# The opening of a two-block transformer kernel: conditioning weights loaded at once and made the stationary operand, normalized tiles scaled by two engines, their transposes placed between the groups of the first projection

## What is computed

```
mod_x = silu(c)     @ w_ada[l] + b_ada[l]      # 1024 -> 6 * 1024, for the tokens
mod_c = silu(c_ctx) @ w_ada[l] + b_ada[l]      # the same for the context
sh1, sc1, g1, sh2, sc2, g2 = split(mod, 6)
h_x = layer_norm(x)   * (1 + sc1) + sh1
h_c = layer_norm(ctx) * (1 + csc1) + csh1
p_x = h_x @ w_in                               # 1024 -> 544 + 1280 + 3 * 1024 columns
p_c = h_c @ w_in
```

## Time and profile before

| | us |
|---|---|
| median of 3 runs | 3383.12 |
| lowest and highest | 3379.35, 3383.62 |
| the profiled execution, its device time | 3381.08 |
| its span in the profile | 3379.0 |
| PE busy (x15388 matmuls) | 3080.0 (91%) |
| DVE busy | 2036.5 (60%) |
| ACT, POOL busy | 1028.9, 1001.6 (30% each) |

### The profile page before, as it was taken

One profiled execution on the slowest core, in us unless ns is written; L12 is line 12 of the kernel. 1 busy time (PEld: TensorE's weight loads), 2 busy tenths in 40 slices (PEclk: granted clock), 3 DMA queues, 4 the chain that ended last, 5 costly groups with the idle time before them and its releaser, 6 DMA issues.

```text
span 3379.0 us, 38543 instructions
## 1 busy us (share of the span) xinstructions
PE 3080.0 (91%) x15388; PEld 2491.5 (74%) x15388; DVE 2036.5 (60%) x3032; ACT 1028.9 (30%) x1799; POOL 1001.6 (30%) x754
## 2 busy tenths in 40 slices
PE   6998889999999999989899998899998887989798
PEld 3985767888488888869576676588878866787576
DVE  4576775555665555482677554666665856667354
ACT  3125773000231112131367200322222135421352
POOL 1003776552210000010078675200001135531262
PEclk9999999999999999989899999899998988999799
DMA  6411003433322121123101466132212310122100
GB/s 206 154 57 29 10 29 94 111 107 111 112 75 75 50 75 52 73 64 137 28 1 38 127 178 209 50 117 100 100 50 94 110 50 1 39 76 101 50 1 25
DMA packets 206353, 267.76 MB, mean 79 GB/s; under 512 B 29296, under 2 KB 133696, under 8 KB 205536
## 3 DMA queue, kind: packets, MB, share of 16 engines
q1 hardware_dynamic: 204096, 265.30, 24.4%
q10 hardware_dynamic: 2080, 0.01, 0.0%
HBM read 254.65 MB, written 10.52 MB: 78 GB/s over the span
## 4 chain that ended last, share of the span: by engine, by line
PE 38%; DVE 6%; ACT 2%; issue 2%; POOL 2%; DMA 1%; SPq 0%; DVEq 0%; POOLq 0%
PE ps L373 14%; PE ps L2010 5%; PE ps L2020 4%; PE ps L2500 2%; PE ps L1329 2%; PE ps L1792 1%; PE ps L1312 1%; PE ps L2830 1%; PE ps L1282 1%; PE ps L1094 1%; PE ps L2775 1%; DVE U L2945 1%; PE ps L3184 1%; DVE U L1439 0%; PE ps L3136 0%
## 5 line engine op out<-in xcount | busy, mean ns | idle before, releaser
L752 POOL TENSOR_TENSOR ht_lo<-HT,ht_hi 128x1024 fp32r<-128x1024 f32 x28 | 67.6, 2415 | 1075.0 <-DVE X L710 629.5
L2010 PE MATMUL ps<-ht_hi,w_hi 128*128 128x512 f32 (+1 forms) x832 | 286.9, 345 | 18.5 <-POOL ht_lo L752 9.8
L2010 PE MATMUL ps<-ht_lo,w_hi 128*128 128x512 f32 (+1 forms) x832 | 285.8, 343 | 0.0
L2010 PE MATMUL ps<-ht_hi,w_lo 128*128 128x512 f32 (+1 forms) x832 | 285.6, 343 | 0.0
L2020 PE MATMUL ps<-w_hi,a_hi 128*128 128x512 f32 x640 | 251.0, 392 | 4.3 <-DVE a_lo L2135 4.3
L2020 PE MATMUL ps<-w_lo,a_hi 128*128 128x512 f32 x640 | 249.9, 390 | 0.0
L2020 PE MATMUL ps<-w_hi,a_lo 128*128 128x512 f32 x640 | 249.7, 390 | 0.0
L373 PE MATMUL ps<-w_lo,ht_hi 128*128 128x320 f32 (+2 forms) x800 | 245.8, 307 | 0.0
L1496 POOL TENSOR_TENSOR p_lo<-ring,p_hi 128x512 fp32r<-128x512 f32 x156 | 199.9, 1292 | 102.7 <-DVE p_hi L1451 78.1
L595 DVE SCALAR_TENSOR_TENSOR U<-U,stat 128x512 f32<-128x512 f32 x224 | 218.8, 977 | 12.1 <-DMA U<-w_ada_dram 2.4
L373 PE MATMUL ps<-gate_ht_hi,gate_w_hi 128*128 128x512 f32 (+1 forms) x576 | 213.7, 371 | 12.1 <-POOL w_lo L1678 6.4
(11 more groups left out here) (427 smaller groups left out, 8232.9 us busy)
## 6 DMA issues: line engine op xcount, KB each, us to landing
ring<-w_dram SPq DMA_DIRECT2D x30, 2048.0 KB, 7.9
U<-w_ada_dram SPq DMA_DIRECT2D x80, 512.0 KB, 3.6
ring<-w_in_dram SPq DMA_DIRECT2D x48, 512.0 KB, 6.5
ring<-w_in_dram SPq DMA_DIRECT2D x8, 1280.0 KB, 6.0
ring<-a_w_in_dram SPq DMA_DIRECT2D x8, 1280.0 KB, 6.7
ring<-w_ada_dram SPq DMA_DIRECT2D x4, 2048.0 KB, 10.6
hi_scratch<-ht_hi SPq DMA_DIRECT2D x2, 3072.0 KB, 10.0
gate_ht_hi<-hi_scratch SPq DMA_DIRECT2D x8, 768.0 KB, 4.6
```

The source lines that it names most:

```text
L752: pool.tensor_tensor(HT_LO[:, :, tokens], HT[:, :, tokens], HT_HI[:, :, tokens].bitcast(F32), ALU.subtract).then_inc(ht_ready.sem, 1)
L2010: last = pe.matmul(ps[:, g % 4, 0:c1 - c0], lhsT, rhs, start=(k + j == 0), stop=(k == KD - 1 and j == 2))
```

## The change

`w_ada[0]`'s four blocks go to four places in `U` (`ADA_W`) and are asked for at the start, ahead of `w_in`; `ctx` is asked for between the second and the third. The weights become the stationary operand: for each of 16 blocks of 128 output columns, eight matmuls with the two columns of `sil` as the moving operand (new line 514), whose sums stand as columns in PSUM at once. The copies and the 16 small transposes go. The biases are added first (`ada_biases`). Tiles 0 and 1 are transposed between the blocks, tiles 2 to 5 ahead of groups 0 to 3 of A0. ACT scales the first four of a tile's eight feature pieces and DVE the other four (`place_half`, new line 818), interleaved with the splitting of A0's and A1's weights. `XNS` moves, so that the projection's output doesn't overwrite it. In `gemm` the units of `Macs` shift by one slot for the projection: unit u has its `pieces` behind the split of slot u+1 and its `pe` after group 0 of slot u+2, and what is left over stands behind the projection. Line numbers after line 217 differ by 2 to 32.

```diff
-        def gemm(G, mms, evac, depth, ..., pieced=None):
+        def gemm(G, mms, evac, depth, ..., pieced=None, beside=None):
-                                if macs and g == (2 if G == 3 else 1):
-                                    macs.pe(pe, i * 2 + s - 1)
+                                if macs and g == (2 if pieced else 1):
+                                    macs.pe(pe, i * 2 + s - (1 if pieced else 2))
...
+                                if beside:
+                                    beside(eng, i * 2 + s, 0)
                                 eng.wait_ge(ring_full[s].sem, i * (16 * parts) + ring_full[s].n + 16 * parts)
                                 for q in range(pieces):
+                                    if beside and q:
+                                        beside(eng, i * 2 + s, q)
...
                                 if macs and name[s] == "vector":
-                                    macs.take(eng, i * 2 + s - 1)
-                                    macs.pieces(eng, i * 2 + s, 0, 4)
+                                    macs.take(eng, i * 2 + s - 2)
+                                    macs.pieces(eng, i * 2 + s - 1, 0, 4)
...
-        MODROW = U[0:2, 6 * D:8 * D]
+        ADA_W = [view(at, KD, 512) for at in (8448, 12544, 4096, 0)]
...
+                    for c in range(4):
+                        if c == 2:
+                            sp.dma_start(X[:, XT:NT, :], A["ctx"]...).then_inc(ctx_loaded.sem, 16)
+                        sp.dma_start(ADA_W[c], rows(A["w_ada"][0])[:, :, c * 512:(c + 1) * 512]).then_inc(ada_loaded[c].sem, 16)
                     first_loads(sp, lambda s: None)
-                    sp.dma_start(X[:, XT:NT, :], A["ctx"]...).then_inc(ctx_loaded.sem, 16)
...
+        def ada_first(p):
+                    pe.wait_ge(sil_ready.sem, 1)
+                    for c in range(4):
+                        if c >= 2:
+                            turn_tile(pe, p, c - 2, XNS[:, c - 2, :], 2 * (c % 2))
+                        pe.wait_ge(ada_loaded[c].sem, 16)
+                        for j in range(4 * c, 4 * c + 4):
+                            for k in range(KD):
+                                last = pe.matmul(ps[:, 5, 2 * j:2 * j + 2], ADA_W[c][:, k, j % 4 * P:(j % 4 + 1) * P],
+                                                 sil[:, k, :], start=(k == 0), stop=(k == KD - 1))
+                    last.then_inc(mod_turned.sem, 1)
...
-        XNS = view(0, NT, D)
+        XNS = view(27984, NT, D)
...
-                        place_tile(act, p, 0, 0, t, 2 * (t % 2))
+                        place_tile(act, p, 0, 0, t, 2 * (t % 2), HALF)
+                        act.wait_ge(half_placed.sem, t + 1)
                         round_tile(act, p, t)
...
+        def place_half(dve, p, t):
+            dve.wait_ge(mod_ready.sem, 1)
+            dve.wait_ge(turn_done.sem, p.turned + t + 1)
+            for k in range(HALF, KD):
+                last = dve.tensor_scalar(HT[:, k, tokens], ps[:, 2 * (t % 2) + k // 4, k % 4 * P:(k % 4 + 1) * P],
+                                         modc[:, 0, KD + k, who:who + 1], modc[:, 0, k, who:who + 1], ALU.mult, ALU.add)
+            last.then_inc(half_placed.sem, 1)
...
             if macs:
+                macs.pe(nc.tensor, 2)
+                macs.take(nc.vector, 2)
+                macs.pieces(nc.vector, 3, 0, 4)
                 macs.pe(nc.tensor, 3)
                 macs.take(nc.vector, 3)
                 macs.all_taken(nc.tensor)
...
             def ready(pe, g):
+                if l == 0 and g + 2 < NT:
+                    pe.wait_ge(half_placed.sem, g + 1)
+                    turn_tile(pe, now, g + 2, XNS[:, g + 2, :], 2 * (g % 2))
                 pe.wait_ge(ht_ready.sem, now.ht + g + 1)
```

More of the change, by code:

```diff
@@ L217, in build @@
         bias_loaded = signal("bias_loaded")
+        ada_loaded = [signal(f"ada_loaded{c}") for c in range(4)]
+        half_placed = signal("half_placed")
         sil_ready = signal("sil_ready")
@@ L316, in first_loads, with gemm @@
                         d.then_inc(ring_full[s].sem, 16)
-        def gemm(G, mms, evac, depth, split=None, join=True, ready=None, loads=None, macs=None, behind=None, between=None, pieced=None):
+        def gemm(G, mms, evac, depth, split=None, join=True, ready=None, loads=None, macs=None, behind=None, between=None, pieced=None, beside=None):
             n, parts, issue = streams[at_stream[0]]
@@ L726, in place_tile @@
             act.wait_ge(turn_done.sem, p.turned + t + 1)
-            for k in range(KD):
+            for k in range(n):
                 last = act.activation(HT[:, k, tokens], ps[:, bank + k // 4, k % 4 * P:(k % 4 + 1) * P], ACT.Identity,
@@ L804, in first_ht, with half_beside, piece, project @@
             return p
+        def place_half(dve, p, t):
+            who = 0 if t < XT else 1
+            tokens = slice(t * P, (t + 1) * P)
+            dve.wait_ge(mod_ready.sem, 1)
[4 more added lines that the diff above has]
+            last.then_inc(half_placed.sem, 1)
+        def half_beside(p):
+            before = {0: (0,), 1: (1,), 3: (2,)}
+            def piece(dve, u, q):
+                if u == 0:
+                    for t in before.get(q, ()):
+                        place_half(dve, p, t)
+                if u == 1 and q == 0:
+                    for t in range(3, NT):
+                        place_half(dve, p, t)
+            return piece
         HT_HI = rounded_view("ht_hi", "U", at_ot, KD, T)
         PROJECT_W = [rounded_view(f"project_w_hi{s}", "U", at_xn + D + s * KD * 320, KD * 320) for s in range(SLOTS)]
-        def project(nt, width, col, dst, join=True, ready=None, macs=None):
+        def project(nt, width, col, dst, join=True, ready=None, macs=None, beside=None):
             def mms(s, g, d):
```

36 lines of the change are left out of this document (10 added, 26 removed).

## The result

| | median us (range) | ratio to before, 95% interval |
|---|---|---|
| before | 3381.23 (3373.94 to 3383.62) | |
| changed kernel | 3402.55 (3399.78 to 3405.98) | 1.0066 [1.005, 1.0082] |
| forecast | 3411, range 3380 to 3418 | |

The change makes the kernel slower by 21 us. The profiled executions say the same: 3400.7 us of span against 3379.0, +21.7. The forecast's sum was +28.8.

The account below looks back on a forecast made before the run. The prediction took the opening as one chain: conditioning product, scales, six tiles, projections. 24.3 - 6.9 + 11.4 = +28.8 on 3381.1 gave 3409.9; going halfway to a median 2.0 higher, it said 3411 us, range 3380 to 3418.

Parts of the forecast that it names:

- The conditioning product and the clock: Opening: product with stationary weights takes 54.5 us at 1.2 GHz, so the scales come 24.3 us later.
- R: Moment the conditioning scales are ready, end of the addition at line 522; forecast 74.3 us.
- Both choices: Conditioning product: the clock stays at 1.2 GHz throughout, and a record there takes 0.213 us, not 0.106.
- Rival W: Conditioning product: weight load doesn't slow at 1.2 GHz; scales at 48.8, sum +3.4, 3385 us; chance 0.06.
- F: As a rival: two-column records cost less, conditioning product 18 us, sum -6.4, 3375 us; chance 0.05.
- H: Rival: the clock rises during the conditioning product; scales at 46.9, sum +1.5, 3383 us; chance 0.26.
- Tiles, A0 and A1: From the scales to A1's end: earlier A0 start, four tiles' transposes inside A0; 6.9 us better than before.
- E - R: Time from the scales to A1's end (B0's first matmul); forecast 48.1 us, before 55.0.
- the lost cover: A0: DVE places tile 3 behind a split piece waiting with POOL for SBUF; 0 to 3 us more.
- B0 to B3: Later projection slots: B1's stall goes, B3's stall and unit 3's exposed tail come; 112.8 us, or +11.4.
- F - E: Time from B0's first matmul to the Fourier mix's first matmul; B0 to B3 forecast +11.4 us.
- Rival T: Behind B3: unit 3 isn't exposed, taking 16.7 us off; 3394 with low clock, 3367 with high; chance 0.06.

Follow-up runs that it names:

- e3: Changed kernel with eight wide 512-column matmuls added on PE ahead of the conditioning product; 3401.5 us, ratio 1.0062 to the kernel before.
- e7: Changed kernel with 128 instead of two moving columns in the conditioning product; 3378.5 us, ratio 0.9996 to the kernel before.
- e8: Changed kernel without DVE's half of the scaling, ACT scaling all eight pieces of each tile; 3403.6 us, ratio 1.0079 to the kernel before.
- e1: Changed kernel with the old order of the four `Macs` units beside B0 to B3 put back; 3392.7 us, ratio 1.0029 to the kernel before.
- e5: Changed kernel with PE's run ahead of group 1 again in layer 0's gated stage; 3409.4 us, ratio 1.0095 to the kernel before.
- e6: Kernel before with only PE's run moved ahead of group 2 in layer 0's gated stage; 3374.5 us, ratio 0.9983 to the kernel before.
- e4: Changed kernel with the old `Macs` order, except unit 0's pieces behind B1's split on DVE; 3385.1 us, ratio 1.0019 to the kernel before.
- e10: Changed kernel with conditioning weights moving, eight wide matmuls ahead, and unit 0's pieces behind B1's split; 3363.1 us, ratio 0.9952 to the kernel before.

## Why the prediction was right, and where it was not

*The side and the range* were right: slower by 0.66%, inside 3380 to 3418. The 3411 was 8.5 too high.

*The conditioning product and the clock*, +24.3: R was 73.81 where I had 74.3. Both choices that it hung on held, and the experiments show them rather than only agree: the record is 0.107 us at 2.4 GHz and 0.21 at 1.2 (e3), and the level was 1.2 with two moving columns and 2.4 with 128, all else alike (e7). Rival W is out by e3, and F with it. (The forecast's R for W, 48.8, doesn't come out of its own terms: 15.5 + 27.2 + 3.9 + 0.4 is 47.0, which makes the sum of that case +1.6 and not +3.4. Nothing hung on it.) H was the true alternative, and the distance that the forecast put between the two cases at R, 27.4, is 24.6 in e7, with 0.114 instead of 0.106 a record.

*Tiles, A0 and A1*, -6.9: E - R is 49.3 by B0's first matmul, against 54.8 before, so -5.5. A0 began 5.2 behind R (I had 5.9). The difference is a wait that I had carried over: before, ACT began 0.9 after R, because tile 0's transposes stood behind the scales; now they are done long before, and ACT begins at once:

```profile
73.84 1.51 ACT L735 ACTIVATE HT<-ps,modc 128x128 f32<-128x128 f32 x4 [43.44 <-DVE modc L522]
```

But A0 and A1 then took 44.2, where the forecast's terms give 41.9 by the same landmark (37.6 before, and 4.3). Of that, 1.8 are the waits of 1.40 and 0.41 for DVE's weight pieces, which stand behind the tiles that it scales. The piece behind the first wait also runs beside POOL's work on the tiles and takes 1.71 + 2.79 us, where the pieces around it take 0.43 + 0.72:

```profile
77.52 1.71 DVE L405 CAST project_w_hi<-ring 128x544 fp32r<-128x544 f32 x1
79.12 2.36 POOL L759 TENSOR_TENSOR ht_lo<-HT,ht_hi 128x1024 fp32r<-128x1024 f32 x1 [0.19 <-ACT ht_hi L744]
79.26 2.79 DVE L409 TENSOR_TENSOR w_lo<-ring,project_w_hi 128x544 fp32r<-128x544 f32 x1
```

About 1 us more is the clock: some 22 matmuls of A0 ran at 1.2 GHz, at 0.23 instead of 0.13 us each, and 12 before. Against these stands that tile 2's transposes came ahead of A0's first group, so only three tiles' fell inside. I had named the lost cover and put it at 0 to 3, and the clock at up to 3 more, and set nothing for either in the sum. e8 shows that the engine added there gives back what it brings.

*B0 to B3*, +11.4, counted to the restart in the Fourier mix: F - E grew by 10.6, and 1.8 came behind F at the low clock (30.7 at the first copy, less 28.9 at F), 12.4 in all. Term by term: the stall at B1 went; the one at B3 came, 4.0 of waiting for 3.5 forecast and by the mechanism forecast, the ring's load behind the loads of `w_ada`; unit 3 was exposed with a wait of 12.94 for 12.6; the last run took 3.58 instead of 1.84, 1.7 more as forecast. e1 confirms the whole part from the other side.

*Up to here* the sum was to be +28.8 and is +30.7 at the first copy of the Fourier mix, so the forecast was 1.9 too low: -0.4 at R, +1.4 in A0 and A1, +1.0 in B0 to B3.

*The missing term.* The sentence "a shift of the end of B3 is a shift of the end of the kernel" was true only if nothing else had changed, and something had: the step that failed is the reading of one line of the diff, `g == (2 if pieced else 1)`, which the forecast took as belonging to the projections alone. In the gated stage of layer 0 it moves PE's run from ahead of group 1 to ahead of group 2 and saves 5.8 us of slots in the profiled pair (277.7 to 271.9): DVE's result that frees a PSUM bank for the next slot comes 1.5 us sooner, and PE's waits for it shrink from 6.5 to 2.3 us. e5 puts the line back and the kernel is 6.8 slower; e6 makes it alone and the kernel before is 5.9 faster. With this term the sum would have been 28.8 - 5.8 = 23.0, against the 21.7 of the profiled pair.

*What stays open* is the remaining 3 us between the gated stage and the end. The lateness wanders between 16 and 26 us there in code that is the same, and it wanders in the other kernels too. TensorE's clock differs there: its mean from 2500 to 3000 us is 0.90 in the kernel before and 0.92 in the changed one. No run shows whether that is the cause.

*Rival T*, the tail that isn't paid, did not come: the wait of 12.94 stands in the trace in full.

## What to carry to other kernels

A busy engine is not a fast one: look at the spacing of equal instructions against the same instruction elsewhere. Matmuls that were nearly all weight load (two moving columns against 128 weights) ran at half of TensorE's clock for 58 us, and lost a high clock that was given to them; reading the same columns 64 times over cost 0.007 us a record and took 24.6 us off.

When a pipeline is shifted by one step to take a stall out, count what stands behind the last step: the stall of 7.7 went and 13 us of an uncovered unit came. Reordering only the one step that stood in the way (e4) took the stall without the tail.

Follow each changed condition to every caller. A line of this change that looked like a rewording was worth as much as all that was done for the tiles.

## What the runs showed of the hardware that I had not expected

In e3 the granted clock fell from 1.00 to 0.50 at 18.7 us, with PE busy for the 2.9 us before and idle for the 2.25 ahead of these, and it stayed at 0.50 through 52 us of two-column matmuls and two tiles' transposes without a gap. I had expected it not to rise; that a high level is lost within 2.9 us of such a stream no row of the kernel before had shown. With the same pause and 512-column matmuls behind it, it stayed at 1.00 (e10).

Matmul records with 128 x 128 f32 weights and two moving columns, back to back, stand 0.107 us apart at 2.4 GHz and 0.21 at 1.2; with 128 moving columns they stand 0.114 apart at 2.4. Up to there the columns are almost free.
